# Two attention stages of a fp32 block pair on one core: another order of the weight chunks, value matmuls on the two column halves, and high and low parts side by side in the stationary operand

## What is computed

```python
# first block, 8 heads of 64: softmax attention and stick-breaking attention
outs.append(jnp.einsum('bhqk,bhkd->bhqd', w.astype(vb.dtype), vb))
...
outs.append(jnp.einsum('bhqk,bhkd->bhqd', a.astype(vb.dtype), vb))
# second block, compressed keys and values: blocks of 32 tokens, stride 16, through a small network
return jax.nn.silu(flat @ w1) @ w2
# its queries and gates, and its three branches
qg = h @ w_qg
gates = jax.nn.sigmoid(qg[..., N_HEADS * HEAD_DIM:].astype(jnp.float32))
...
o = gt[..., 0:1] * o_c + gt[..., 1:2] * o_s + gt[..., 2:3] * o_w
```

## Time and profile before

| what | value |
|---|---|
| median of 3 runs | 1269.09 us (1266.14 to 1271.99) |
| the profiled execution, its own time | 1267.09 us |
| span in its profile | 1265.2 us |
| PE busy | 1221.0 us, 97% |
| DVE, ACT, POOL busy | 881.3, 648.5, 229.5 us |
| granted TensorE clock, mean | 0.986 |

### The profile page before, as it was taken

One profiled execution on the slowest core, in us unless ns is written; L12 is line 12 of the kernel. 1 busy time (PEld: TensorE's weight loads), 2 busy tenths in 40 slices (PEclk: granted clock), 3 DMA queues, 4 the chain that ended last, 5 costly groups with the idle time before them and its releaser, 6 DMA issues.

```text
span 1265.2 us, 19851 instructions
## 1 busy us (share of the span) xinstructions
PE 1221.0 (97%) x7930; PEld 1082.9 (86%) x7930; DVE 881.3 (70%) x1220; ACT 648.5 (51%) x855; POOL 229.5 (18%) x116
## 2 busy tenths in 40 slices
PE   5999999999999999999999999999989889999996
PEld 4888889986889988888999988888989758888885
DVE  5877766785977787766778776655687654866554
ACT  6555545560655665544543465544455663655441
POOL 1443200002000043420000025500000240355000
PEclk9999999998999999999999999999999989999998
DMA  6555555450724465555445555555557202555540
GB/s 262 204 196 197 183 190 193 169 200 34 200 75 154 161 220 193 178 195 199 167 164 184 195 175 201 183 197 198 212 191 255 78 34 69 188 190 188 198 166 34
DMA packets 31041, 217.34 MB, mean 172 GB/s; under 512 B 3408, under 2 KB 3584, under 8 KB 5488
## 3 DMA queue, kind: packets, MB, share of 16 engines
q1 hardware_dynamic: 29616, 210.66, 47.2%
q0 software_dynamic: 1344, 5.53, 1.7%
HBM read 215.10 MB, written 4.22 MB: 173 GB/s over the span
## 4 chain that ended last, share of the span: by engine, by line
PE 87%; DVE 7%; ACT 3%; issue 2%; POOL 0%; DMA 0%; DVEq 0%; SPq 0%; ACTq 0%
PE bank L1386 38%; PE bank L1387 19%; PE bank L1379 7%; PE bank L1381 7%; PE bank L1380 7%; DVE w_hl L742 2%; ACT w_hl L390 1%; PE bank L1723 1%; PE bank L1564 1%; PE bank L1442 1%; DVE y_f L1206 1%; PE bank L1443 1%; PE bank L1444 1%; DMA par<-small 0%; PE bank L1450 0%
## 5 line engine op out<-in xcount | busy, mean ns | idle before, releaser
L742 DVE TENSOR_TENSOR w_hl<-raw,w_hl 128x2048 fp32r<-128x2048 f32 x197 | 450.7, 2289 | 119.5 <-ACT w_hl L390 118.7
L390 ACT ACTIVATE w_hl<-raw 128x2048 fp32r<-128x2048 f32 x197 | 375.0, 1908 | 128.0 <-PE bank L1381 69.4
L1386 PE MATMUL bank<-x_hl,w_hl 128*128 128x512 f32 x864 | 302.8, 397 | 12.8 <-DVE w_hl L917 12.8
L1386 PE MATMUL bank<-hidden,w_hl 128*128 128x512 f32 x864 | 299.7, 394 | 0.0
L337 POOL TENSOR_TENSOR hidden<-hid_f,hidden 128x256 fp32r<-128x256 f32 (+1 forms) x76 | 189.5, 2493 | 530.1 <-ACT hidden L477 310.3
L1387 PE MATMUL bank<-x_hl,w_hl 128*128 128x256 f32 x864 | 240.5, 278 | 0.0
L1387 PE MATMUL bank<-hidden,w_hl 128*128 128x256 f32 x864 | 239.3, 277 | 0.0
L1386 PEld LDWEIGHTS bank<-x_hl,w_hl 128*128 128x128 f32 x864 | 163.1, 189 | 50.7 <-issue 12.8
L1386 PEld LDWEIGHTS bank<-hidden,w_hl 128*128 128x128 f32 x864 | 162.0, 188 | 37.6
L1379 PE MATMUL bank<-x_hl,w_hl 128*128 128x256 f32 x576 | 166.4, 289 | 1.0 <-DVE x_hl L759 0.6
L1380 PE MATMUL bank<-x_hl,w_hl 128*128 128x256 f32 x576 | 164.3, 285 | 0.0
(11 more groups left out here) (318 smaller groups left out, 1604.5 us busy)
## 6 DMA issues: line engine op xcount, KB each, us to landing
raw<-weights SPq DMA_DIRECT2D x198, 1024.0 KB, 4.8
bias_skew<-bias_rows POOLq DMA_DIRECT2D x1, 3072.0 KB, 23.3
gate_or_bias<-bias_skew POOLq DMA_DIRECT2D x1, 2048.0 KB, 10.9
h<-x_t SPq DMA_DIRECT2D x1, 1024.0 KB, 4.9
out_t<-x_f SPq DMA_DIRECT2D x4, 256.0 KB, 2.1
con<-consts SPq DMA_DIRECT2D x1, 672.5 KB, 12.3
heads<-p_t POOLq DMA_DIRECT2D x1, 256.0 KB, 3.2
par<-small SPq DMA_DIRECT2D x1, 199.5 KB, 5.2
```

Of the source, the lines that this page charges most:

```text
L390: nc.scalar.activation(w_hi[:, s, :], raw[:, s, :], ACT.Copy).then_inc(hi_split, 1)
L742: V.tensor_tensor(w_lo[:, s, :], raw[:, s, :], w_hi[:, s, :].bitcast(F32), ALU.subtract).then_inc(lo_split, 1)
L1386: mm(out_, w_hi[:, s, c:c + m], x, start=start, stop=False, **kw)
```

## The change

1. The chunks of the sparse attention come in another order: query 0, gates, query 1, the two key chunks of phi, query 2, the two value chunks of phi, query 3. PE, ACT and DVE follow, so DVE writes the values' blocks later and in two pieces, and `blocks` writes both key pairs in one instruction instead of two.
2. Gates and phi hold high and low part side by side in one stationary operand 128 wide (gates: 64 columns of each in `w_hi`; phi: 64 of each in `blk_k`, `blk_v`), so two matmuls stand where three stood, and the lower half of the result has to be added: ACT copies it (`g_low`, `phi_low`) and DVE adds it (L1257 and L1274 of the changed kernel). The gates' chunk is packed in 512 instead of 1024 columns and its split covers those alone, instead of 2048.
3. In the first attention, the values of the stick-breaking attention go to the other 64 partitions, and `om` and `os` alternate. `om` now waits for `s_a` too, and `m_pv` is counted once, at the end. The rows of `w_branch_sb` are exchanged to fit.
4. In the loop, ACT copies both parts of a transposed pair right after the first head's exponentials, DVE puts `n_factors` between the two `n_tops`, ACT splits the first two output chunks ahead of the loop, and DVE the last of these in turn 8 instead of 4.

```diff
-          ("kv_raw", 2), ("k_att", 2), ("nsa_q0", 1), ("nsa_gate", 1), ("phi", 4), ("nsa_q", 3), ("v_att", 2),
-          ("nsa_out", 4), ("mlp1", 2 * MF)]
+          ("kv_raw", 2), ("k_att", 2), ("nsa_q0", 1), ("nsa_gate", 1), ("nsa_q1", 1), ("phi_k", 2),
+          ("nsa_q2", 1), ("phi_v", 2), ("nsa_q3", 1), ("v_att", 2), ("nsa_out", 4), ("mlp1", 2 * MF)]
...
-                nc.scalar.activation(w_hi[:, s, :], raw[:, s, :], ACT.Copy).then_inc(hi_split, 1)
+                dst, src = w_hi[:, s, :], raw[:, s, :]
+                if c is not None and c == C["nsa_gate"]:
+                    dst, src = gate_parts(s)[0], gate_parts(s)[2]
+                nc.scalar.activation(dst, src, ACT.Copy).then_inc(hi_split, 1)
...
-            hi(blk_h[:, 0, 0:960], y_flat[:, 0:960], blk_ready, 4)
-            nxt(C["nsa_q0"])
-            hi(blk_h[:, 1, 0:960], y_flat[:, 960:1920], blk_ready, 8)
+            hi(blk_k[:, :, 0, 0:60], by_l(y_flat[:, 0:960]), blk_ready, 4)
+            nxt(NSA_Q[0])
+            act.wait_ge(chunk_used, C["nsa_gate"] + 1)
+            nc.scalar.activation(second[0:48, 0, 0, :], bank[64:112, 2, 0:S], ACT.Copy).then_inc(g_low, 1)
             nxt(C["nsa_gate"])
-            nxt(C["phi"])
+            nxt(NSA_Q[1])
             act.wait_ge(g_tr, 1)
             nc.scalar.activation(nsa_g[:, :, :], bank[:, 5, 0:96].rearrange("p (a b) -> p a b", a=2),
                                  ACT.Sigmoid).then_inc(g_sig, 1)
+            nxt(PHI[0])
+            hi(blk_v[:, :, 0, 0:60], by_l(y_flat[:, 960:1920]), blk_ready, 8)
             def phi_gate(w):
-                act.wait_ge(chunk_used, C["phi"] + 2 * w + 2)
+                act.wait_ge(chunk_used, PHI[2 * w + 1] + 1)
+                nc.scalar.activation(phi_second[:, w, :], bank[64:124, PHI_BANK[w], 0:256], ACT.Copy).then_inc(phi_low, 1)
+                act.wait_ge(phi_full, w + 1)
                 if w == 1:
                     act.wait_ge(phi_hid, 1)
-                nc.scalar.activation(t_exp[0:60, :], bank[0:60, PHI_BANK[w], 0:256], ACT.Sigmoid).then_inc(phi_sig, 1)
+                nc.scalar.activation(t_exp[0:60, :], phi_sum[:, w, :], ACT.Sigmoid).then_inc(phi_sig, 1)
             phi_gate(0)
-            nxt(C["phi"] + 1)
-            nxt(C["phi"] + 2)
+            nxt(PHI[1])
+            nxt(NSA_Q[2])
+            nxt(PHI[2])
             phi_gate(1)
...
-            def n_copies(t, e):
-                act.wait_ge(n_pt, 2 * t + e + 1)
+            def n_copies(t):
+                act.wait_ge(n_pt, 2 * t + 1)
                 if t >= 2:
                     act.wait_ge(n_pv, t - 1)
-                if e == 0:
-                    nc.scalar.activation(nsa_t[:, t % 2, 0, 0:512], bank[:, 5, :], ACT.Copy).then_inc(n_ptc, 1)
-                elif t % 2 == 0:
+                nc.scalar.activation(nsa_t[:, t % 2, 0, 0:512], bank[:, 5, :], ACT.Copy).then_inc(n_ptc, 1)
+                if t % 2 == 0:
+                    act.wait_ge(n_pt, 2 * t + 2)
...
-            for j in range(1, 4):
-                nxt(NSA_Q[j])
+            nxt(NSA_Q[3])
             n_exps(0)
             n_exps(1)
             v_in(0)
+            nxt(C["v_att"])
...
-            nxt(C["v_att"])
             v_in(1)
+            nxt(C["v_att"] + 1)
             for t in range(2, PAIRS + 2):
-                for e in range(2):
-                    if t < PAIRS:
-                        n_exps(2 * t + e)
-                    n_copies(t - 2, e)
+                if t < PAIRS:
+                    n_exps(2 * t)
+                n_copies(t - 2)
+                if t < PAIRS:
+                    n_exps(2 * t + 1)
...
-                if t == 4:
-                    nxt(C["v_att"] + 1)
...
-                        for t in range(2):
...
+                        V.tensor_tensor(dst[:, :, e:4:2, :], src[:, :, :, half:half + NCMP],
+                                        pe[rows, :].rearrange("p (l a n) -> p l a n", a=1, n=1).to_broadcast(
+                                            [64, 16, 2, NCMP]), ALU.add).then_inc(blk_ready, 1)
...
-            lo(blk_l[:, 0, 0:960], y_flat[:, 0:960], blk_h[:, 0, 0:960])
-            blocks(1, (0, 1))
...
-            dve.wait_ge(chunk_used, C["nsa_gate"] + 1)
-            V.tensor_tensor(t_a[0:48, :], bank[0:48, 2, 0:S], r_sb[0:48, :], ALU.mult).then_inc(g_raw, 1)
+            dve.wait_ge(g_low, 1)
+            st.done(V.tensor_tensor(t_a[0:48, :], bank[0:48, 2, 0:S], second[0:48, 0, 0, :], ALU.add))
+            V.tensor_tensor(t_a[0:48, :], t_a[0:48, :], r_sb[0:48, :], ALU.mult).then_inc(g_raw, 1)
             nxt(C["nsa_gate"])
-            lo(blk_l[:, 1, 0:960], y_flat[:, 960:1920], blk_h[:, 1, 0:960])
-            nxt(C["phi"])
+            blocks(1, (0,))
+            query(1)
+            nxt(NSA_Q[1])
+            blocks(1, (1,))
+            nxt(PHI[0])
+            lo(blk_v[:, :, 1, 0:60], by_l(y_flat[:, 960:1920]), blk_v[:, :, 0, 0:60])
...
+                dve.wait_ge(phi_low, w + 1)
+                V.tensor_tensor(phi_sum[:, w, :], bank[0:60, PHI_BANK[w], 0:256], phi_second[:, w, :],
+                                ALU.add).then_inc(phi_full, 1)
+                dve.wait_ge(phi_full, w + 1)
                 dve.wait_ge(phi_sig, w + 1)
-                V.tensor_tensor(phi_h[:, w, :], bank[0:60, PHI_BANK[w], 0:256], t_exp[0:60, :],
-                                ALU.mult).then_inc(phi_hid, 1)
+                V.tensor_tensor(phi_h[:, w, :], phi_sum[:, w, :], t_exp[0:60, :], ALU.mult).then_inc(phi_hid, 1)
             phi_silu(0)
-            nxt(C["phi"] + 1)
-            nxt(C["phi"] + 2)
+            nxt(PHI[1])
+            query(2)
+            nxt(NSA_Q[2])
+            nxt(PHI[2])
             phi_silu(1)
+            nxt(PHI[3])
...
-                    n_tops(2 * t + 1)
                 if t - 1 < PAIRS:
                     n_factors(t - 1)
+                if t < PAIRS:
+                    n_tops(2 * t + 1)
                 n_copies(t - 2)
...
-                if t == 4:
+                if t == PAIRS:
...
+                    pe.wait_ge(s_a, g + 1)
                     om, mt = bank[r, ob, 0:S], m_t[g % 2]
-                    mm(om, mv[:, 0, cols], mt[:, 0:256], start=True, stop=False).then_inc(m_pv, 1)
-                    mm(om[:, 128:256], mv[:, 1, cols], mt[:, 256:384], start=False, stop=True).then_inc(m_pv, 1)
-                    pe.wait_ge(s_a, g + 1)
-                    os, sp_ = bank[r, ob, S:2 * S], s_p[g % 2]
-                    mm(os, sv[:, 0, cols], sp_[:, 0:256], start=True, stop=False)
-                    mm(os[:, 128:256], sv[:, 1, cols], sp_[:, 256:384], start=False, stop=True).then_inc(s_pv, 1)
+                    os, sp_ = bank[64 - 64 * (g % 2):128 - 64 * (g % 2), ob, S:2 * S], s_p[g % 2]
+                    mm(om, mv[:, 0, cols], mt[:, 0:256], start=True, stop=False, **kw)
+                    mm(os, sv[:, 0, cols], sp_[:, 0:256], start=True, stop=False, **kw)
+                    mm(om[:, 128:256], mv[:, 1, cols], mt[:, 256:384], start=False, stop=True, **kw).then_inc(m_pv, 2)
+                    mm(os[:, 128:256], sv[:, 1, cols], sp_[:, 256:384], start=False, stop=True, **kw).then_inc(s_pv, 1)
...
-                last = product(bank[:, 2, 0:S], c % RING, k * P, P, y_hl[:, k, :, :], k == 0, k == KT - 1)
+                both = w_hi[:, c % RING, P * k:P * k + P]
+                mm(bank[:, 2, 0:S], both, y_h[:, k, :], start=k == 0, stop=False)
+                last = mm(bank[:, 2, 0:S], both, y_l[:, k, :], start=False, stop=k == KT - 1)
             last.then_inc(chunk_used, 1)
-            for w in range(2):
+            pe.wait_ge(kv_done, 3)
+            query(1)
+            pe.wait_ge(g_raw, 1)
...
+            ins.then_inc(g_tr, 1)
+            def compress(w):
+                pe.wait_ge(op_lo, PC["blk_k"] + w + 1)
                 for half in range(2):
-                    c = C["phi"] + 2 * w + half
+                    c = PHI[2 * w + half]
                     arrived(c + 1)
-                    if half == 0:
-                        pe.wait_ge(op_lo, PC["blk_k"] + w + 1)
-                        pe.wait_ge(setup, 7)
                     for l in range(8):
...
+                        o = bank[:, PHI_BANK[w], 0:256]
+                        both = (blk_k, blk_v)[w][:, 8 * half + l, :, :].rearrange("p a b -> p (a b)")
                         wh, wl = (t[:, c % RING, l * 256:l * 256 + 256] for t in (w_hi, w_lo))
-                        mm(o, blk_h[:, w, a:a + 120], wh, start=half == 0 and l == 0, stop=False)
-                        mm(o, blk_h[:, w, a:a + 120], wl, start=False, stop=False)
-                        last = mm(o, blk_l[:, w, a:a + 120], wh, start=False, stop=half == 1 and l == 7)
+                        mm(o, both, wh, start=half == 0 and l == 0, stop=False)
+                        last = mm(o, both, wl, start=False, stop=half == 1 and l == 7)
                     last.then_inc(chunk_used, 1)
...
-                    ins.then_inc(g_tr, 1)
-            query(1)
```

(34 more changed lines are left out.)

48 lines of the change are left out of this document (24 added, 24 removed).

## The result

The changed kernel takes 1255.5 us (median of 4, 1254.51 to 1257.37), the kernel before in the same session 1268.1 us (4 runs, 1266.14 to 1271.99). The ratio is 0.990, with a 95% interval of 0.9878 to 0.9923: 12.6 us less, where 14.5 us were forecast (1254.5 against a median of 1269.09 then). Measured once more it took 1254.98 us, ratio 0.9903 (0.9876 to 0.9929).

What follows compares the result with a forecast made beforehand. PE was taken as the bound (busy 1221.0 of 1265.2 us), with DVE and latencies between four engines bounding the sparse attention. -3.6 - 4.1 - 7 = -14.7, rounded to -14.5, gave a 1254.5 us median; 8-in-10 range 1248.5 to 1260.5.

Steps and rivals of the forecast that it cites:

- Part 1: First attention: value matmuls on column halves overlap, saving 0.66 us a head in six of eight; -3.6 us, between 0 and -4.6.
- The new wait for ACT: First attention: `om` waits 0.6 us for `s_a` in the first head; PE also waits in the last; both savings lost.
- Part 2: Sparse attention's first part: DVE's row decides, the first value chunk starts at 976.8 instead of 980.87; -4.1 us.
- The walk of DVE's row: Sparse attention's first part: DVE's instructions followed from 933.7, giving PE's start of the first value chunk at 976.8.
- of the 4.8 us of matmuls and the 4.21 us hole about half comes out: Sparse attention's first part: of 9.0 us together about half is gained; four smaller waits, 6.6 us, replace the hole.
- Part 3: Sparse attention's loop: PE's work stays, holes shrink and the clock recovers; -7 us, between 0 and -12.
- Holes: Sparse attention's loop: PE's waits for DVE, ACT and POOL fall from 9 us to 5, between 2 and 9.
- the split in turn 8: Sparse attention's loop: DVE's split moved to where only copies stand behind it, removing a 2.6 us hole.
- The clock: Sparse attention's loop: shorter holes bring back 3 us of 5 us lost to the low clock, between 0 and 5.
- the loop keeps its pace: Rival, sparse attention's loop: POOL takes over the other waits, clock unchanged, only the 2.6 us hole goes; 1259 us, 17%.
- The sum: Whole kernel: -3.6 - 4.1 - 7 = -14.7, rounded to -14.5 us; median forecast 1254.5 us.

Runs made afterwards that it cites:

- e3: The kernel before with only the new column-half value matmuls of the first attention added; 1265.39 us, ratio 0.9973.
- e2: The changed kernel with the first attention's old four value matmuls and old packing of `w_branch_sb` restored; 1255.53 us, ratio 0.9891.
- e2b: e2 measured again: the changed kernel with the old value matmuls and `w_branch_sb` packing; 1258.12 us, ratio 0.9926.
- e7: The changed kernel with a third matmul put back beside each pair of gates and phi (40 more, results wrong); 1253.85 us, ratio 0.9879.
- e8: The changed kernel with phi/query 3 splits before the first phi sum and sigmoid, DVE's last key-value split after its copy, turn 8's split behind the loop; 1246.31 us.
- e4: The changed kernel with ACT's copies, DVE's factors and both value-chunk splits back at their old places in the loop; 1258.83 us, ratio 0.9926.
- e5: The changed kernel with ACT's and DVE's splits for phi's second value chunk and query 3 ahead of the first phi sum and sigmoid; 1258.97 us.

## Why the prediction was right, point by point

**Part 1, -3.6.** Measured: -3.4 (before to changed, and e3), -4.0 and -3.4 (e2, e2b). The column halves overlap, as the earlier trace rows suggested. The new wait for ACT came in the first and the last head, as named, and a little in the second: 1.57 us of wait instead of 0.78 in the first, 0.15 in the second, 1.01 instead of 0.18 in the last.

**Part 2, -4.1.** PE's start of query 0 to the first value chunk went from 47.16 us to 43.29, -3.9, and to 42.73, -4.4, in the second profile. The walk of DVE's row gave waits of 1.8, 2.9, 0.8 and 1.1 us; the second profile has 1.5, 2.7, 0.7 and 1.0. (The first lacks the last two: PE ran at the low clock behind the 2.70 us wait and came late of itself.) The merged block instruction takes 1.01 us, forecast 1.06. Wrong was one sentence of the account: "of the 4.8 us of matmuls and the 4.21 us hole about half comes out". The matmuls gave nothing (e7), and the merged block instructions shortened DVE's row by 0.6 us (2.25 to 2.03 and 4.47 to 4.05). The narrower split of the gates' chunk does not show in it: DVE takes up the split behind the drain 2.01 us after query 0's start in both kernels (935.72 and 932.03), when ACT's half is done. What is left of the gain, over 3 us, is the order's by elimination; the new order alone was not run. The side-by-side form begins to pay only in e8's order.

**Part 3, -7.** Measured by D -5.8, by e4 -6.7, of which 2.9 and 2.5 us are waits and the rest is clock. Holes: 9.0 to 6.1 us, forecast 5. The term that was off is the split in turn 8, which I had costed at nothing "where only copies stand behind it": true for DVE, but the multiply beside it on POOL pays 2.05 us. The clock: of 70.96 us at a mean of 0.90, 7.1 us are missing to full speed, of 65.18 at 0.95, 3.3 us, so by this estimate 3.8 us came back; PE's busy time fell by 2.8 us (61.92 to 59.14), and with the 2.9 us of holes that makes the 5.8 of D. Forecast 3. That it came out so near is in part luck: the same loop with the same waits had 0.95 in three profiles, 0.92 in two and 0.88 in e5, and in e5 nothing came back (63.46 us busy). The rival "the loop keeps its pace" is ruled out by two waits: ACT's copy 3.2 us to none, DVE 3.7 to 0.8. POOL took over in part, as the prediction said it would.

**The sum.** -14.7 forecast; -12.7 in the spans of the two profiled executions (1265.2 to 1252.5): A -0.3, B -3.4, from B's end to DVE's drain -0.7 (the later drain of before, told above), C -3.2, D -5.8, E +0.6. The mechanisms held; two sizes were off: the split in turn 8, 2 us, and in part 2 the share given to the matmuls, which paid nothing.
